# A hybrid decoder step on one core: transfers of x ahead of the first weights, VectorE's late work in pieces, taps by a plan, the conformer norm later

## The reference

```python
def token_mixer(xn, ...):                       # xn = rmsnorm(h)
    proj = xn @ w_in                            # 1536 qkv, 512 z, 4 + 4 a and b, 2 x 512 glu
    qkv_c = silu(causal_dwconv([qkv_buf, qkv], conv_qkv_w))     # 4 taps
    q, k, v = l2norm(q) / sqrt(128), l2norm(k), v
    g, beta = -exp(a_log) * softplus(a + dt_bias), sigmoid(b)
    o = gated delta rule over q, k, v, g, beta  # chunks of rows, one after the other
    o = rmsnorm(o, gdn_norm_w) * silu(z)
    glu = glu_in[:, :512] * sigmoid(glu_in[:, 512:])
    c = causal_dwconv([conf_buf, glu], conf_dw_w) + conf_dw_b   # 31 taps, 512 channels
    c = silu(layernorm(c, conf_ln_w, conf_ln_b))
    return concat([o, c]) @ w_out, new states
h = h + token_mixer(rmsnorm(h));  h = h + peer_ffn(rmsnorm(h));  y = rmsnorm(h)
# peer_ffn: 8 heads, two top-16 of 128 keys each, a top-16 of the sums, 16384 experts of one neuron
```

## Time and profile before

| | us |
|---|---|
| median of 3 runs | 1883.71 (1883.66 to 1886.05) |
| the profiled execution's own time | 1889.95 |
| its span | 1888.2 |
| PE busy in the span | 1802.2 (95%) |
| DVE busy | 1393.0 (74%) |
| ACT busy | 712.0 (38%) |
| mean granted TensorE clock | 0.975 of full speed |

### The profile page before, as it was taken

The page is one execution under the profiler, slowest core; times in us unless marked ns, Lnnn a source line. Parts: engine busy times, 40 slices in busy tenths (PEclk is TensorE's granted clock), DMA queues, the critical chain, the costliest instruction groups (busy, mean ns, idle before and its releaser), DMA issues.

```text
span 1888.2 us, 29407 instructions
## 1 busy us (share of the span) xinstructions
PE 1802.2 (95%) x11505; PEld 1752.5 (93%) x11505; DVE 1393.0 (74%) x2528; ACT 712.0 (38%) x1244; POOL 672.4 (36%) x438
## 2 busy tenths in 40 slices
PE   6997879799899999999999999999999999999998
PEld 5997779789899999999999999999999999999997
DVE  4876896565499999999966657526878788887753
ACT  4535333642333343334344333333333333333332
POOL 3000000000000467868777677771344333333100
PEclk9988899889999999999999999999999999999999
DMA  7211001045132368888998989999999999999831
GB/s 209 68 45 45 32 1 52 1 100 151 41 112 90 126 238 277 266 294 298 321 312 302 314 291 308 316 329 403 322 387 379 348 341 359 357 340 345 318 115 37
DMA packets 190706, 424.33 MB, mean 225 GB/s; under 512 B 11162, under 2 KB 119222, under 8 KB 180320
## 3 DMA queue, kind: packets, MB, share of 16 engines
q1 hardware_dynamic: 153256, 287.47, 44.0%
q0 software_dynamic: 37312, 134.97, 20.4%
HBM read 360.76 MB, written 62.06 MB: 224 GB/s over the span
## 4 chain that ended last, share of the span: by engine, by line
PE 59%; DVE 15%; issue 2%; POOL 1%; ACT 0%; DMA 0%; DVEq 0%; POOLq 0%
PE psum L1292 31%; PE psum L1271 21%; PE psum L1259 3%; PE psum L901 3%; DVE junk L2395 2%; DVE besti L2258 1%; DVE sring L2262 1%; DVE besti L2270 1%; DVE best L2266 1%; DVE best L2254 1%; PE psum L906 1%; DVE oh L2385 1%; DVE WR L1786 1%; DVE eqx L2322 1%; DVE pick L2333 1%
## 5 line engine op out<-in xcount | busy, mean ns | idle before, releaser
L1271 PE MATMUL psum<-xT,WS 128*128 128x416 f32 x3072 | 595.0, 353 | 4.6 <-POOL WS L841 4.6
L1292 PE MATMUL psum<-AR,WS 128*128 128x416 f32 x3072 | 580.5, 350 | 2.6 <-DVE AR L2466 2.6
L1292 PEld LDWEIGHTS psum<-AR,WS 128*128 128x128 f32 x3072 | 574.2, 187 | 8.9 <-DVE AR L2466 3.0
L1271 PEld LDWEIGHTS psum<-xT,WS 128*128 128x128 f32 x3072 | 572.1, 188 | 10.6 <-POOL WS L841 6.2
L841 POOL TENSOR_TENSOR WS<-RAWP,WS 128x1024 fp32r<-128x1024 f32 x128 | 309.7, 2430 | 720.8 <-ACT WS L1686 620.2
L906 PE MATMUL psum<-xT,WR 128*128 128x280 f32 (+1 forms) x1968 | 282.2, 304 | 15.0 <-DVE ss L1795 7.8
L832 POOL DMA_INDIRECT rowg<-in_expert_v,idx x128 | 182.5, 1426 | 315.4 <-DVE acc L2409 307.6
L906 PEld LDWEIGHTS psum<-xT,WR 128*128 128x128 f32 x1968 | 270.4, 200 | 16.7 <-DVE ss L1795 8.1
L1696 ACT ACTIVATE WS<-RAWP 128x1024 fp32r<-128x1024 f32 x128 | 135.6, 1059 | 332.5 <-PE psum L1292 332.5
L2459 DVE TENSOR_TENSOR WS<-RAWP,WS 128x1024 fp32r<-128x1024 f32 x128 | 156.7, 1224 | 114.6 <-ACT WS L1696 114.6
L1723 ACT ACTIVATE actA<-psum 128x416 f32<-128x416 f32 x128 | 66.4, 519 | 404.9 <-PE psum L1271 404.6
(11 more groups left out here) (373 smaller groups left out, 1610.2 us busy)
## 6 DMA issues: line engine op xcount, KB each, us to landing
RAWP<-in_expert_u SPq DMA_DIRECT2D x64, 1024.0 KB, 6.8
RAWP<-in_expert_v SPq DMA_DIRECT2D x64, 1024.0 KB, 7.9
act_dram<-actA SPq DMA_DIRECT2D x128, 208.0 KB, 4.3
gate_dram<-gblk SPq DMA_DIRECT2D x26, 1024.0 KB, 10.4
act<-act_dram SPq DMA_DIRECT2D x64, 416.0 KB, 8.3
Gt<-gate_dram SPq DMA_DIRECT2D x16, 1664.0 KB, 9.7
RAW<-in_w_in SPq DMA_DIRECT2D x8, 1024.0 KB, 5.4
RAW<-in_w_query SPq DMA_DIRECT2D x8, 1024.0 KB, 8.4
```

The source lines that it names most:

```text
L1271: last = mm(bank[e % 2][:, 0:TD], ws(e)[:, pw, kt * P:(kt + 1) * P], xT[:, px, kt, TSP:TPE], start=(kt == 0 and i == 0), stop=(kt == KT - ...
L1292: last = mm(bank[dt][:, 0:TD], ws(NK + e)[:, pw, dt * P:(dt + 1) * P], AR[:, e % 4, pa, :], start=(e == 0 and i == 0), stop=(e == NK - 1 a ...
```

## The change

- SP issues all five tiles of x before the weights of block 0, which stood behind tile 2. ACT and DVE take tile 3's steps ahead of the first split of weights. GpSimd issues the two small loads (`dtb`) first and waits for tile 4's arrival before it issues the two large states `sconf` and `sqkv`.
- Block 7: `row_squares`, the first half of `row_scales`, and the roots on ACT come inside it, and PE's norm matmuls behind its second unit in place of its fourth. The five taps behind it go, and the silu of its channels moves ahead of the next weight split on ACT.
- In the late part a `low(b)` is four instructions of 512 elements (`late_lows`) at places of their own, 1.5 apart; `conformer_seqs` is split into two halves of the product (`seqs_product`) and the sum (`seqs_sum`), a place apart, behind the gate (`late_glus`).
- `feed` follows a plan: `due(at_)` is the number of taps that are to be done by a place, at most 3 at a time.
- The conformer norm moves from places 46 to 49.6 to 48.5 to 52.8, its squares get places of their own, and the `onb` and `on` steps of three output tiles move 1.7 to 2 places back.

```diff
-CONV_BY = {2: 5, 3: 10, 4: 16, 5: 21, 6: 26, 7: CC}
+CONV_BY = {2: 5, 3: 10, 4: 16, 5: 21, 6: 26}
...
-        NORM_AT = {"ls": 46, "lc": 46.05, "lv0": 47.1, "lv1": 47.6, "lv2": 48.1, "lv3": 48.6, "lr": 48.7,
-                   "lm": 49.1, "ln": 49.6}
+        NORM_AT = {"ls": 48.5, "lc": 48.55, "sq0": 49.3, "sq1": 49.35, "lv0": 50.3, "lv1": 50.8, "sq2": 50.85,
+                   "lv2": 51.3, "sq3": 51.32, "lv3": 51.75, "lr": 51.85, "lm": 52.3, "ln": 52.8}
...
             for t in range(NTB):
                 load_rows(t)
-                if t == 2:
-                    load_weights(0)
+            load_weights(0)
...
+                if n == 8:
+                    pool.wait_ge(x_in[NTB - 1], 16)
                 pool.dma_start(dst, src).then_inc(small_in, 16)
...
             for b in range(1, LATE):
-                linear(b)
-                scalars(b)
+                if b == LATE - 1:
+                    linear(b, lambda n: scalars(LATE - 1) if n == 1 else None)
+                else:
+                    linear(b)
+                    scalars(b)
...
-            def conformer_seqs(c):
+            def seqs_product(c, q0, q1):
...
+            def seqs_sum(c):
...
-            def late_blocks():
+            def late_lows():
+
+                for b in range(LATE + 1, first["out"] - 1):
+                    n = sum(x[2] for x in BLOCKS[b + 1][2])
+                    for i in range(4):
+                        yield ("lin", 2 * (UNIT0[b] - UNIT0[LATE]) + 1.6 + 1.5 * i), LIN
+                        A.wait(dve, "high", b + 1)
+                        k = slice(2 * i, 2 * i + 2)
+                        op(tt(WR[:, (b + 1) % 2, 1, k, 0:n], RAW[:, SLOT[b + 1], k, 0:n],
+                              WR[:, (b + 1) % 2, 0, k, 0:n].bitcast(F32), ALU.subtract), "low", b + 1)
+
+            def late_glus():
 
                 for b in range(LATE, first["out"]):
-                    k = 2 * (UNIT0[b] - UNIT0[LATE])
-                    if b == LATE:
-                        yield ("lin", k + 1.1), LIN
-                        row_scales()
-                    if b + 1 < first["out"] and b > LATE:
-                        yield ("lin", k + 1.2), LIN
-                        low(b + 1)
                     if BLOCKS[b][0] == "glu":
+                        k, c = 2 * (UNIT0[b] - UNIT0[LATE]), BLOCKS[b][1]
                         yield ("lin", k + 8.5), LIN
                         glu(b)
+                        yield ("lin", k + 9.9), LIN
+                        for i in range(2):
+                            if i:
+                                yield ("lin", k + 10.9), LIN
+                            seqs_product(c, 4 * i, 4 * i + 4)
+                        yield ("lin", k + 11.9), LIN
+                        seqs_sum(c)
...
+            def due(at_):
+
+                return 26 + int(min(max(at_ - 5, 0), 5) + 2 * min(max(at_ - 9.6, 0), 18.4)
+                                + 2.6 * min(max(at_ - 28, 0), 12) + 3.2 * max(at_ - 40, 0))
+
             def feed(at_):
 
-                conv_to(min(pieces[0] + (2 if at_ < LINEAR_END else 1), CC * gated[0]))
+                conv_to(min(max(pieces[0], due(at_)), pieces[0] + 3, CC * gated[0]))
```

More of the change, by code:

```diff
@@ L1422, in _ @@
             xhigh(1, 1)
-            high(0)
-            xhigh(1, 2)
             square(1, 4)
             root(1, 4)
+            xhigh(1, 2)
+            high(0)
             xhigh(1, 3)
@@ L1459, in _ @@
                 evacuate(b)
-                while done < 2 * sum(x[0] == "qkv" for x in BLOCKS[:b]):
+                if b == LATE - 1:
+                    V.wait(act, "qk2")
+                    fn(tok[:, RQ], tok[:, RQ], ACT.Sqrt)
+                    fn(tok[:, RK], tok[:, RK], ACT.Sqrt, "rqk")
+                while done < 2 * sum(x[0] == "qkv" for x in BLOCKS[:b + (b == LATE - 1)]):
                     silu(done)
@@ L1473, in late_blocks @@
                         evacuate_unit(b, u)
-                        if k == 0:
-                            V.wait(act, "qk2")
-                            fn(tok[:, RQ], tok[:, RQ], ACT.Sqrt)
-                            fn(tok[:, RK], tok[:, RK], ACT.Sqrt, "rqk")
-                        if k == 1:
-                            silu(2 * HEADS + 2)
-                            silu(2 * HEADS + 3)
                         if u == UNIT0[b + 1] - 1 and b + 2 < first["out"]:
@@ L1613, in norm_tile_conf @@
                 for c in range(NG):
-                    yield f"lv{c}", NORM
+                    yield f"sq{c}", NORM
                     V.wait(act, "lc", c)
@@ L1861, in row_scales @@
                     op(dve.tensor_scalar(tok[:, i, LAST4], of_chunks(bank[7], lo), EPS, None, ALU.add), "qk2")
+            def row_scales():
                 A.wait(dve, "rqk")
@@ L1913, in _ @@
             xlow(1, 1)
+            xnorm(1, 3)
+            xlow(1, 2)
             low(0)
-            xlow(1, 2)
-            xnorm(1, 3)
             xnorm(1, 4)
@@ L1933, in qkv_conv @@
                 for c in (2 * i, 2 * i + 1):
+                    if b == LATE - 1 and c % 2:
+                        row_squares()
                     e = c % 2
```

27 lines of the change are left out of this document (15 added, 12 removed).

## The result

The changed kernel takes 1871.38 us in the median (four runs, 1868.36 to 1873.6), the kernel before 1883.91: the ratio is 0.9932, with a 95% interval of 0.9904 to 0.9961.

The account below looks back on a forecast made before the run. The prediction took the mixer's length, with PE's waits and low clock in its late stretches, to set the time. Terms of -4.0, -9.0, -12.4, +2.4 and -7.0 gave -30.0 from the 1883.71 us median: 1853, range 1838 to 1872.

Parts of the forecast that it names:

- Term 1: Prologue: x loaded ahead of block 0's weights and the states lets PE start earlier, -4.0 us.
- Term 2: Seam and chunk 0, to chunk 1's `gb`: PE's norm wait mostly moved, partly won, with a better clock, -9.0 us.
- Term 3: Chunk 1's `gb` to its `ws`: 20 fewer taps on DVE and no wait for `M`, -12.4 us to 60.
- Term 4: Chunk 1's `ws` to chunk 2's: DVE gets 14 more taps and becomes the bound, +2.4 us to 66.
- Term 5: Chunk 2's `ws` to the output blocks: waits for the norm's squares go, its burst costs 2.5, -7.0 us.
- Rival A: DVE becomes the bound in the middle, terms 4 and 5 at their upper ends: 1871 us (1864 to 1880), chance 0.14.
- the second: Sign of a wrong prediction: the last stretch, chunk 2's `ws` to the output blocks, isn't shorter than 109 us.
- The first: Sign of a wrong prediction: DVE's share in the fourth stretch comes with waits of 5 us and more.
- the third: Sign of a wrong prediction: the granted clock falls below 0.8 again behind the seam.

Follow-up runs that it names:

- e0: The kernel before, run once more with no edit as a control: 1885.5 us, ratio 1.0016.
- e1: The kernel before with only the prologue's part of the change: 1880.1 us, ratio 0.998.
- e8: The changed kernel with block 7 as before (five taps ahead of the norms, roots and factors in the late part): 1869.9 us, ratio 0.9924.
- e7: The changed kernel with splits, product and sum in one piece again at their old places, the plan of taps kept: 1881.3 us, ratio 0.9983.
- e4: The changed kernel with the old feed of taps instead of the plan; pieces and moved norm stay: 1899.0 us, ratio 1.0075.
- e14: e9 with no taps between chunk 1's `ws` and chunk 2's `gb`, six more before chunk 1's `gb`: 1860.7 us, ratio 0.9845.
- e11: The changed kernel with the 44 taps between chunk 1's `ws` and chunk 2's `ws` left out: 1858.4 us, ratio 0.9845.
- e6: The changed kernel with the norm's end (reciprocals and scalings) in pieces at places of their own: 1866.6 us, ratio 0.9906.
- e3: The kernel before with prologue, block 7's part and the pieces, but the old feed and old norm places: 1900.5 us, ratio 1.0084.
- e12: The changed kernel with the last 15 taps, behind chunk 2's `ws`, left out: 1866.0 us, ratio 0.9873.
- e9: e6 with five more taps done early, in blocks 2 to 6: 1862.1 us, ratio 0.9885.

## Why the prediction was wrong

The sign, the range (1838 to 1872, just) and the first half hold; the size does not. By the first pair of profiles the five terms came to -4.5, -8.8, -17.6, +9.2 and +1.9, -19.8 in sum where -30.0 was forecast (-14.2 against e0, near the 12.5 by time). Terms 4 and 5 were 15.7 us short of the forecast, and terms 1 and 3 hid 5.7 of it. By its own steps:

**Term 1, -4.0:** PE's first unit came 4.36 us earlier and the long row of blocks 4.49. By e1 2.5 us are left in time and 3.8 of it in the profile at G0. The part that goes, goes while PE is busy throughout: in 100 to 140 us it never idles in either kernel, and the granted clock was 0.87 before and 0.83 after:

```profile
100.00:140.00 40.00, 40.00 (x272) 39.48 (x272) 28.15 (x51) 14.90 (x39) 0.00 (x0) 0.83 0.09 27
```

The term was right but for that. sconf landed 7.1 us after its issue (11.1 before), and W0 was there when ACT came to it at 17.31, without a wait. The rule of the Trainium skill ("DMA: Bandwidth & Descriptors", "Queues, rings and completion order"), by which each DMA engine takes turns between its queues, allowed a delay of W0 that would have left 2.6 of the 4.0 us; this case's trace shows no such delay, by the 17.31 and by PE's first unit at 19.68.

**Term 2, -9.0:** in sum right by the first profile (-13.3 at chunk 1's `gb`, 4.5 of it from the prologue: -8.8), and 3 less by e0. The size was right by luck, for the mechanism was wrong. "The wait of 4.57 is thus mostly moved, and 3.6 of it won": e8 keeps the wait and reaches chunk 1 sooner. The wait of 3.61 for `KH` came as forecast; but DVE's `gb` was 2.6 us earlier only, 1.9 less than the prologue gave, and the gain lies behind it, in 25.2 instead of 35.9 us. That stretch is 34.6 to 36.1 in every kernel with the old feed, 28.9 without the pieces (e7) and 27.2 without the seam (e8): mostly feed and pieces made it short.

**Term 3, -12.4:** -17.6, inside the bound of 52 us. DVE's 47.3 us of work were forecast to the us (48). The 11 us that I left above PE's work were 7. Shown by e4 and e7: the same kernel needs 76.6 us with the old feed and 63.0 without the pieces.

**Term 4, +2.4: the step that failed.** "Now DVE is the bound, nearly without cover. I take 66, 3.7 above DVE's work." DVE's work was as counted (60.9, forecast 62.3), but the stretch took 72.8. I had treated DVE as a bound that acts when it is full. It acts at the handovers: taps that stand ahead of a chunk's step delay it, up to 2.4 us for three. PE waits 4.5 us for chunk 2's `KH` alone, behind half products, a sum, two quarters and six taps, and e14, which takes only the taps away, ends that wait. e11 puts the price at 9 to 12.7 us for 44 taps. A second part is missing from the term altogether: 5.0 us of PE's own work came into this stretch and left the next one (65.53 x 0.93 = 60.9 us at full clock, before 55.9). The 9.2 us are thus 5.0 of work and 5.8 more of idle time (7.3, before 1.5), less 1.6 that the low clock cost less.

**Term 5, -7.0: the other.** +1.9, and +4.8 against e0. "-7.6 - 2 + 2.5": the waits for squares did go, but the move of the norm by itself, with no tap behind W2, gave 1.2 us (e4's 105.2 against 106.4 in e0) to 5.5 (against 110.7 in e3), and 0.9 to 1.5 of idle time; its end in one burst costs 5.2 (e6, 4.4 of it idle time) where I had 2.5, and it fell on chunk 3's last step before it fell on chunk 4. And the 15 taps, which I said would "stand between steps of two chunks, one or two at a time" and put at nothing, cost 3.5 (e12) to 6.0 (e4). Against e0, -1.2 and +6.0 make the +4.8. The stretch is longer than before although 5.1 us of PE's work had left it (86.17 x 0.85 = 73.2, before 78.3): PE idles 25.0 us where it idled 18.3. Over the last two stretches PE's work is the same as before, and its idle time has grown by 12.5 us, which is more than the 11.1 that they gave back.

**The base.** The differences were taken from a profile that was 6 us above the median, and "I apply them to the median" carried its low clock and its longer wait at the seam along: by e0, 5.7 us of before's 435.6 up to the output blocks were that execution's own.

Rival A had the time (1871) and half of the mechanism: term 4 above its upper end (+9.2 for +8.4) and term 5 above the 0 that A gave it (+1.9). It expected DVE to be full, which it isn't in any of the four stretches (86% at most, from G1 to W1), and a poor term 3, which was the best one; so its hitting the time is in part luck. I gave it 0.14 since I looked at DVE's mean share and not at where its instructions stand.

Of the three signs by which the prediction was to be known as wrong, the second came (the last stretch is 111.2 and not under 109). The first came in sum only (PE idles 7.3 us in the fourth stretch, its longest wait there is 4.46), and the third didn't (behind the seam the granted clock is 0.93).

## What to carry to other kernels

An engine that takes filler work (the taps) is not free until it is full: filler ahead of a handover is paid, here with 0.2 to 0.7 us for an instruction of 0.8 by the stretches' lengths, and 0.14 to 0.37 by PE's idle time. Filler put where PE is busy throughout cost nothing that was seen (e9, five taps). Where filler is dealt out by places, cutting other work into pieces adds places and thus filler (e3, +16 us); a plan by count takes this away, and only then are the pieces worth their 10 us. A wait that a profile names can be worth nothing (e8): before counting it, ask when the next engine could have used the result. And a stretch that gets shorter or longer may only have passed work to its neighbour: compare PE's work and its idle time, and not lengths alone.
